# The z half of an input projection: five column groups with three sets of split weights, or four equal groups with one set split slice by slice

## The reference

```python
def in_project(h, w_in, pos):
    z = h @ w_in
    q = rope(z[..., :OFF_KV_CMP].reshape(B, T, N_HEADS, HEAD_DIM), pos)
    ...                       # keys of three branches: rope; values: as they are
    gates = jax.nn.sigmoid(z[..., OFF_GATE:OFF_POOL].astype(jnp.float32)).astype(h.dtype)
    u = z[..., OFF_POOL:]     # 512 columns, for the pooling branch
```

## Time and profile before

| what | us |
|---|---|
| median of 3 runs | 3094.58 (3092.32 to 3098.67) |
| the profiled execution | 3091.68 |
| its span, first to last instruction | 3089.9 |
| the projection stage in it | 1245.6 to 1468.8 |
| z part of the stage on PE | 1323.1 to 1461.5 |
| mean granted TensorE clock | 0.954 of full |

### The profile page before, as it was taken

One profiled execution on the slowest core, in us unless ns is written; L12 is line 12 of the kernel. 1 busy time (PEld: TensorE's weight loads), 2 busy tenths in 40 slices (PEclk: granted clock), 3 DMA queues, 4 the chain that ended last, 5 costly groups with the idle time before them and its releaser, 6 DMA issues. The chain is left out here.

```text
span 3089.9 us, 46643 instructions
## 1 busy us (share of the span) xinstructions
PE 2799.8 (91%) x18032; PEld 2572.8 (83%) x18032; DVE 1456.6 (47%) x2754; ACT 908.2 (29%) x1552; POOL 342.1 (11%) x361
## 2 busy tenths in 40 slices
PE   4999989999999999899678886887999999999997
PEld 4898879999999999799666664333989999999996
DVE  4444437444454444541167675223264444444545
ACT  4656544111111110322256564333041111111102
POOL 3444420000000000000022223110000000000000
PEclk9999999999999999999579898888999999999999
DMA  4223124111112100311201012644231111111101
GB/s 167 85 90 117 59 76 140 41 54 41 41 50 59 41 27 0 119 45 37 73 32 42 32 42 86 221 144 122 84 96 42 41 41 41 54 41 41 54 0 56
DMA packets 169715, 206.46 MB, mean 67 GB/s; under 512 B 11598, under 2 KB 152783, under 8 KB 166698
## 3 DMA queue, kind: packets, MB, share of 16 engines
q1 hardware_dynamic: 161362, 150.70, 15.9%
q0 software_dynamic: 8224, 54.06, 4.8%
HBM read 190.89 MB, written 18.01 MB: 68 GB/s over the span
## 5 line engine op out<-in xcount | busy, mean ns | idle before, releaser
L406 ACT ACTIVATE f_act_gate<-f_act_gate 128x352 f32<-128x352 f32 x132 | 65.8, 498 | 1186.2 <-DVE f_act_gate L463 1186.2
L500 DVE SCALAR_TENSOR_TENSOR trunk<-f_down,trunk 128x352 f32<-128x352 f32 x528 | 275.8, 524 | 207.8 <-PE f_down L104 207.8
L102 PE MATMUL f_up<-f_h_hi,f_gu_hi 128*128 128x352 f32 x1056 | 344.5, 326 | 0.0
L102 PE MATMUL f_gate<-f_h_hi,f_gu_hi 128*128 128x352 f32 x1056 | 344.3, 326 | 0.0
L104 PE MATMUL f_up<-f_h_hi,f_gu_lo 128*128 128x352 f32 x1056 | 342.7, 325 | 0.0
L104 PE MATMUL f_gate<-f_h_hi,f_gu_lo 128*128 128x352 f32 x1056 | 342.5, 324 | 0.0
L102 PE MATMUL f_down<-f_a_hi,f_wd_hi 128*128 128x352 f32 x1056 | 340.6, 323 | 0.0
L103 PE MATMUL f_gate<-f_h_lo,f_gu_hi 128*128 128x352 f32 x1056 | 340.5, 322 | 0.0
L103 PE MATMUL f_up<-f_h_lo,f_gu_hi 128*128 128x352 f32 x1056 | 340.1, 322 | 0.0
L103 PE MATMUL f_down<-f_a_lo,f_wd_hi 128*128 128x352 f32 x1056 | 338.5, 321 | 0.0
L104 PE MATMUL f_down<-f_a_hi,f_wd_lo 128*128 128x352 f32 x1056 | 338.0, 320 | 0.0
(11 more groups left out here) (374 smaller groups left out, 5616.3 us busy)
## 6 DMA issues: line engine op xcount, KB each, us to landing
as_pages<-in_cache_kv_slc_dram SPq DMA_DIRECT2D x192, 128.0 KB, 2.3
f_gu_raw<-in_w_ffn_gate_dram SPq DMA_DIRECT2D x44, 512.0 KB, 4.1
f_gu_raw<-in_w_ffn_up_dram SPq DMA_DIRECT2D x44, 512.0 KB, 5.4
f_wd_raw<-in_w_ffn_down_dram SPq DMA_DIRECT2D x22, 1024.0 KB, 5.0
at_spread<-saved_rows SPq DMA_DIRECT2D x16, 768.0 KB, 4.1
as_pages<-in_cache_kv_slc_dram POOLq DMA_DIRECT2D x64, 128.0 KB, 3.4
in_w_raw<-in_w_in_dram SPq DMA_DIRECT2D x6, 1024.0 KB, 5.0
x_saved<-trunk SPq DMA_DIRECT2D x2, 2112.0 KB, 13.7
```

What stands on the lines that cost most here:

```text
L102: pe.matmul(out, w_hi, x_hi, start=first, stop=False)
L406: act.activation(act_gate[:, b, :], act_gate[:, b, :], ACT.Silu).then_inc(silu_done, 1)
L500: dve.scalar_tensor_tensor(xT[:, m, chunk(c)], down_bank[n % 4][:, 0:CH], 0.5, xT[:, m, chunk(c)], ALU.mult, ALU.add).then_inc(down_free, 1)
```

## The change

- The z columns are cut into four groups of 326 instead of four of 256 and one of 280. Their order starts at column 512: group 2 has 512 to 837, group 3 838 to 1163, group 4 1164 to 1303 and 0 to 185 (two DMAs, two ACT operations per bank), group 5 186 to 511.
- The three sets of split weights (own tiles, room in `z`, room in `trunk`) become one set, `w_hi` and `w_lo`. `high` and `low` are written as 8 instructions, one per slice k. `high(i + 1)` starts when the last unit of group i has used slice k (new semaphore `w_used`), and PE's first unit of a group waits slice by slice.
- `high(i + 1)` stands ahead of the taking of the ninth tile; `low` moves on DVE (below); the maps stand behind the tiles (2, 5), (2, 8), (3, 2), (3, 6) instead of (2, 6), (2, 8), (3, 3), (3, 8).
- The pooling weights and the small sample tiles live in the room of `norm.inv`, so that their DMA is issued once u is taken.
- The ropes and the output DMAs wait for the tiles of the group that holds their last column.

```diff
+    QUARTER = OFF_POOL // 4
+    z_columns = list(range(OFF_CMP, OFF_POOL)) + list(range(OFF_CMP))
...
+    TAKEN = [TT * (i - 1) for i in range(len(GROUPS))]
...
-    maps_behind = {(2, 6): 0, (2, 8): 1, (3, 3): 2, (3, 8): 3}
+    maps_behind = {(2, 5): 0, (2, 8): 1, (3, 2): 2, (3, 6): 3}
...
-        own = [mem.sb(scope, "in_w_" + part, [P, KT, WIDEST], F32R)[:] for part in ("hi", "lo")]
...
-        sets = [own, in_z, own, in_z, own, in_trunk, own]
+        w_hi, w_lo = [mem.sb(scope, "in_w_" + part, [P, KT, WIDEST], F32R) for part in ("hi", "lo")]
...
                     if i:
-                        sp.wait_ge(w_split, i)
-                    sp.dma_start(w_raw[:, :, 0:n], w_view[:, :, start:start + n]).then_inc(w_landed, 16)
+                        sp.wait_ge(w_split, KT * i)
...
+                pool.wait_ge(u_taken, U)
+                pool.wait_ge(inv_turned, 1)
+                pool.dma_start(w_sb[:], w_pool.rearrange("g p n -> p g n")).then_inc(maps_landed, 16)
...
-                    act.activation(sets[i][0][:, :, 0:n], w_raw[:, :, 0:n], ACT.Copy).then_inc(w_hi_done, 1)
+                    n = WIDTHS[i]
+                    act.wait_ge(w_landed, LANDED[i])
+                    for k in range(KT):
+                        if i and k < KT - 1:
+                            act.wait_ge(w_used, (KT - 1) * (i - 1) + k + 1)
+                        elif i:
+                            act.wait_ge(done, last_of[i - 1] + 1)
+                        act.activation(w_hi[:, k, 0:n], w_raw[:, k, 0:n], ACT.Copy).then_inc(w_hi_done, 1)
...
-                        if t == (0 if i != 4 else 2) and i + 1 < len(GROUPS):
+                        if t == TT - 1 and i + 1 < len(GROUPS):
                             high(i + 1)
...
-                    dve.wait_ge(z_taken, TT * (n + 1))
+                    dve.wait_ge(z_taken, TAKEN[max(group_with(off), group_with(off + heads * HD - 1))])
...
                 low(2)
-                for m, c in ((0, 1), (0, 2), (1, 0), (1, 1), (1, 2)):
-                    take_u(1, m, c)
-                low(3)
...
                 for g in range(3):
                     pool_group(g)
-                low(4)
+                low(3)
                 pool_group(3)
                 rope(0)
-                low(5)
+                low(4)
                 rope(1)
                 rope(2)
-                low(6)
+                low(5)
                 rope(3)
                 rope(4)
...
                     for k in range(KT):
+                        if t == 0:
+                            pe.wait_ge(w_split, KT * i + k + 1)
...
+                        if n == last_of[i] and k < KT - 1:
+                            mm.then_inc(w_used, 1)
```

More of the change, by code:

```diff
@@ L1304, in _, with stage_project @@
                         second(*ended(n, SECOND_AFTER))
[L1307 to L1313, removed]
+def stage_project(nc, mem, K, trunk, gain, w_in, z, z_sample, uT, outs, constants, state_pool, w_pool,
+                  pool_scale, out_prompt, out_sample):
+    QUARTER = OFF_POOL // 4
+    z_columns = list(range(OFF_CMP, OFF_POOL)) + list(range(OFF_CMP))
+    GROUPS = [[(OFF_POOL + n, POOL_WIDTH // 2)] for n in (0, POOL_WIDTH // 2)]
+    for first in range(0, OFF_POOL, QUARTER):
+        columns, pieces = z_columns[first:first + QUARTER], []
+        for n in columns:
+            if pieces and n == sum(pieces[-1]):
+                pieces[-1] = (pieces[-1][0], pieces[-1][1] + 1)
+            else:
+                pieces.append((n, 1))
+        GROUPS.append(pieces)
+    WIDTHS = [sum(n for _, n in pieces) for pieces in GROUPS]
+    WIDEST = max(WIDTHS)
+    LANDED = [16 * sum(len(pieces) for pieces in GROUPS[:i + 1]) for i in range(len(GROUPS))]
+    TAKEN = [TT * (i - 1) for i in range(len(GROUPS))]
     UNITS = [(i, m, c) for i in range(2) for m in range(2) for c in range(CHUNKS)]
@@ L1318, in stage_project, with group_with @@
     last_of = [max(n for n, u in enumerate(UNITS) if u[0] == i) for i in range(len(GROUPS))]
+    def group_with(column):
+        return max(i for i, pieces in enumerate(GROUPS) for n, w in pieces if n <= column < n + w)
     ROWS = POOL_STATE + N_SAMPLE
@@ L1342, in stage_project @@
         diff = flat[:, (POOL_STATE + SEQ) * 3:(POOL_STATE + SEQ) * 3 + T]
-        sample = [mem.sb(scope, f"pl_sample{i}", [P, DEC_BATCH, EXT]) for i in range(3)]
+        sample = [norm.inv[:, DEC_BATCH * EXT * i:DEC_BATCH * EXT * (i + 1)].rearrange("p (b n) -> p b n", b=DEC_BATCH)
+                  for i in range(3)]
         banks = [mem.ps(scope, f"in_bank{i}") for i in range(4)]
@@ L1367, in load @@
                 def load(i):
-                    _, start, n = GROUPS[i]
                     if i:
-                        sp.wait_ge(w_split, i)
-                    sp.dma_start(w_raw[:, :, 0:n], w_view[:, :, start:start + n]).then_inc(w_landed, 16)
+                        sp.wait_ge(w_split, KT * i)
+                    at_column = 0
+                    for start, n in GROUPS[i]:
+                        sp.dma_start(w_raw[:, :, at_column:at_column + n],
+                                     w_view[:, :, start:start + n]).then_inc(w_landed, 16)
+                        at_column += n
                 norm.load(sp, gain)
@@ L1398, in _ @@
                     pool.wait_ge(rotated, n + 1)
[L1399 removed]
+                    pool.wait_ge(z_taken, TAKEN[group_with(off + KV_WIDTH - 1)])
                     first = 0 if key != "win" else (SEQ - WINDOW) // P
@@ L1467, in low @@
                 def low(i):
[L1468 to L1471, removed]
+                    n = WIDTHS[i]
+                    for k in range(KT):
+                        dve.wait_ge(w_hi_done, KT * i + k + 1)
+                        dve.tensor_tensor(w_lo[:, k, 0:n], w_raw[:, k, 0:n], w_hi[:, k, 0:n].bitcast(F32),
+                                          ALU.subtract).then_inc(w_split, 1)
                 def take_u(i, m, c):
@@ L1558, in _ @@
                 dve.tensor_copy(inv_col[0:N_SAMPLE, TT - 1:TT], row_bank[0:N_SAMPLE, TT - 1:TT]).then_inc(inv_col_ready, 1)
-                take_u(1, 0, 0)
+                for m in range(2):
+                    for c in range(CHUNKS):
+                        take_u(1, m, c)
+                    if m == 0:
+                        dve.wait_ge(constants_landed, 16 * len(constants))
+                        dve.wait_ge(x_out, 32)
                 low(2)
-                for m, c in ((0, 1), (0, 2), (1, 0), (1, 1), (1, 2)):
-                    take_u(1, m, c)
-                low(3)
-                dve.wait_ge(constants_landed, 16 * len(constants))
                 dve.wait_ge(turned, 1)
-                dve.wait_ge(x_out, 32)
+                dve.wait_ge(inv_turned, 1)
                 dve.wait_ge(u_taken, U)
```

61 lines of the change are left out of this document (27 added, 34 removed).

## The result

The changed kernel takes 3104.05 us (median of 12 runs, 3099.44 to 3107.47). The kernel before, run beside it, takes 3096.74 (12 runs, 3092.32 to 3101.37). The ratio is 1.0023 with a 95% interval of [1.0014, 1.0032]: 7.3 us slower, with an interval of 4.3 to 9.9. The prediction was +6.8 us, 3101.4, in a range of 3096.5 to 3106.5. The time lies in the range, 2.6 above its middle; 2.2 of that is the kernel before, whose median was 3094.58 in the runs that the prediction started from and 3096.74 here.

A forecast was written before the change was run, and what follows sets the result against it. PE bounds the z part; at the stage's start and end DVE and ACT are on the path. Terms -0.9 + 0.7 + 2.9 + 2.5 + 1.6 = +6.8 us on 3094.58 gave 3101.4, range 3096.5 to 3106.5.

The forecast's parts named there:

- Border of groups 2 and 3: Before group 3, PE waits for DVE's low half, queued behind group 2's pooling: +2.9 us, bounds 2.3 and 3.8.
- The clock: PE's idleness at the border of groups 2 and 3 lets its clock fall in most executions: +1.6 us, bounds 0 and 3.3.
- no-fall rival: Same stalls, but PE's clock stays up at the border of groups 2 and 3: +5.2 us, 3099.8, chance 0.27.
- End of the stage: Behind the last tile DVE has two q ropes, delaying the next stage's first load: +2.5 us, bounds 2.4 and 2.8.
- Start: At the stage's start, ACT's eight pieces of group 0's high half delay PE's second sum: +0.7 us, bounds 0.3 and 1.5.
- Columns: In the z part, tiles of 326 pass the same columns in 216 fewer matmuls: -0.9 us, bounds -1.5 and 0.
- Covers: At u to z and the other group borders, PE's other work hides the splits: nothing; under 1 us each if lost.
- more waits: Slice waits cost on each of four borders, or tiles of 326 run slower: +9 to +12 us, chance 0.15.
- nothing seen: The stall is covered by PE running tile work ahead; border at most 0.5: +2.8 us, 3097.4, chance 0.08.
- Faster by the next stage's clock: The shift makes the chip grant full speed in the next stage, 1500 to 1540: -18 us at most, chance 0.08.
- stages untouched by the diff moving by more than 2 us: A sign, set beforehand, that the prediction is wrong: stages outside the diff move by more than 2 us.

The follow-up runs named there:

- experiment 4: Changed kernel plus 14 unused matmuls on PE behind the maps of tile (2, 8), during its wait for DVE; 3100.31 us, ratio 1.0017 to the kernel before.
- experiment 1: Changed kernel with DVE making group 3's low half inside group 2's pooling, ahead of its wait for the maps; 3096.65 us, ratio 1.0003 to the kernel before.
- experiment 5: Kernel before with only DVE's low half of group 3 moved behind the pooling of group 2; 3104.12 us, ratio 1.0034 to the kernel before.
- experiment 11: Changed kernel run once more, unaltered; 3106.05 us from 7 runs, ratio 1.0023 to the kernel before.
- experiment 3: Changed kernel with group 0's high and low halves in one instruction each; 3101.35 us, ratio 1.0026 to the kernel before.
- experiment 10: Changed kernel with low(3) early, q ropes by token parts, group 0 whole, and 28 unused matmuls behind the first u unit; 3090.66 us, ratio 0.9992 to before.
- experiment 2: Changed kernel with q ropes in three token parts, only the ninth tile's part behind the last taking; 3096.65 us, ratio 1.0009 to the kernel before.
- experiment 6: Kernel before with rope 3 made to wait for the last z tile; 3099.0 us, ratio 1.0009 to the kernel before.
- experiment 8: Changed kernel with low(3) early, q ropes by token parts and group 0 split whole; 3096.94 us, ratio 1.0005 to the kernel before.

## Why the prediction held

*Border of groups 2 and 3, +2.9.* Measured 3.0 (12.21 - 9.22, with the clock held up in experiment 4), or 2.8 against the 9.44 of experiment 1. The prediction's own figures, 4.9 less 2.09, give 2.8 and not 2.9. The chain came out link by link: the taking 0.3 late behind ACT's last high piece, the third map's bank emptied from 1358.93, DVE's second half of the pooling 1359.01 to 1360.80 (1.79, as read), one low piece, PE at 1361.44 after 2.54 of idleness against 2.4 forecast. Experiments 1 and 5 show the cause from both sides.

*The clock, +1.6.* Measured 1.5 (13.73 - 12.21), and it fell in all four profiled executions that kept the stall unfilled, and in experiment 5 with its longer one. So the no-fall rival with its 0.27 was given too much. Its precedent, a clock that stood through 2.9 us of idleness in 1244 to 1248, was one execution: in seven of the thirteen profiles the clock is down in the 8 us behind it. The granted clock stood at 1.00 through the first 2 us of idleness and fell afterwards, which is why the time is lost on the work and not on the wait. In one execution it cost 2.6, within the upper bound of 3.3. That the changed kernel's profile shows 1.5 is in part luck.

*End of the stage, +2.5.* 2.60 in the changed kernel, 2.54 alone in the kernel before.

*Start, +0.7.* 0.60 to 0.70 at the second sum in the pairs of profiles with the same dips. But 0.24 to 0.35 is left at the end of A, so as a term of the sum it was 0.4 too high. The lower bound, 0.3, gave the reason: a part falls into the half-clock stretch and is got back. The Trainium skill (VectorE: DVE Perf Modes, section on the TRN2 errata) says that a latency is exposed between instructions and that many small tiles pay it each. Without overlap the start term would have been 1.4 by the prediction's estimate. The trace agrees with a fixed part and not with paying all of it: ACT's eight pieces of 256 took 2.54 against 1.89 in one, and DVE's eight of 326 took 3.35, 0.42 each, under the 0.49 of one piece by itself.

*Columns, -0.9.* This term was mis-sized too. A tile of 326 took 3.59 and not 3.578 (takings of group 3 at 1366.83, 1370.42 and 1374.01), so 36 of them take 129.2: -0.5 against 129.7, within the bounds. Experiment 1's B gives -0.3. Either way the 216 matmuls saved are worth next to nothing.

*Covers.* u to z, groups 0 to 1, 3 to 4 and 4 to 5 were costed at nothing. The list of PE's waits shows none at these borders that before hasn't, and B in experiment 1 leaves no room for them.

Measured terms: 3.0 + 1.5 + 2.6 + 0.3 - 0.5 = 6.9, against 6.8 forecast and 7.3 [4.3, 9.9] in the medians. That forecast and medians agree so closely is partly luck, since the measurement can't tell 5 from 9, and since a start 0.4 too dear and columns 0.4 too cheap cancelled. The mechanism isn't luck: each term is shown by the stage. The rivals "more waits" and "nothing seen" are excluded by G, B and the table. "Faster by the next stage's clock" didn't happen: from 1500 to 1540 the granted clock is 0.50 as before, with PE busy for 39.54 of 40 us.

I wrote that stages untouched by the diff moving by more than 2 us would make me wrong. In the profile pair they moved by 8, so by its own sign the prediction failed there. The sign was badly chosen. Behind the stage the thirteen profiles take from 1621.06 (before) to 1629.17 us (experiment 11), with experiment 3 at 1622.6, though the stages there are the same program in all. Both profiles of the changed kernel lie at the long end, at 1629.1, but the stage's 7.0 already makes up the difference of the medians. The chance goes with the granted clock: in experiment 10 the three slowest of 11 runs (3097.3 to 3098.3) have a mean of 0.953, the three fastest (3088.3 to 3088.9) 0.957, and in experiment 2 the two slowest (3104.3, 3105.1) have 0.950 to 0.951, against 0.955 to 0.956 in the two fastest (3095.0, 3095.3). What moves the clock from run to run no run shows.

## What to carry to other kernels

When weight halves are made finer or follow the tile, look at what the splitting engine has in its program between two of them: one wait of DVE's for PE's last maps, ahead of PE's next operand, cost 4.5 of 7 us here, and moving one call gave 4.3 of it back. Work that followed the last tile before the barrier was paid in full here, so cut it along the axis on which tiles arrive and do all but the last part early. A short idle stretch of PE cost twice here, once as the wait (2.54 us) and once as the slower matmuls behind it (1.5); where the wait can't be removed, matmuls that nobody reads are worth trying, and a gain of 1 or 2 us is read from the stage's own rows, not from the total.

## What the runs showed of the hardware that I had not expected

- To the kernel before, the unused matmuls gave more than the ropes by parts did. At the start of the stage they took 2.4 us off the second sum, against 1.5 by the ropes, and at the changed kernel's border they took off 1.5 us. From 1262 to 1278 the granted clock was 1.00 with them. The Trainium skill (TensorE: Matmul & The Clock Gate, Part 1) says that activity releases the full rate; these two stretches agree.
- The busy time of the profile doesn't tell the clock. From 1500 to 1540 of the changed kernel, in the stage behind, PE is busy for 39.54 of 40 us at 0.50. Its matmuls there have 128 columns and start 0.21 us apart. What keeps the clock down no run here shows:

```profile
1500.00:1540.00 40.00, 39.54 (x191) 38.53 (x191) 6.26 (x6) 3.88 (x9) 0.00 (x0) 0.50 0.00 1
```

- One and the same stall is followed by half-clock stretches of different length: the fall cost 1.4 to 1.6 us in three executions and 2.6 in one. Behind the one-column matmuls the fall comes in six executions of thirteen (before, experiments 1, 2, 5, 6 and 8), at 1.5 us each.
